# The S5 front of an encoder kernel: zero-led Toeplitz strips issued by one queue, the discretisation split over two engines, x loaded in quarters

## The reference

```python
def s5_mixer(u, lam_re, lam_im, log_step, b_re, b_im, c_re, c_im, d, glu_w, glu_b):
    ...
    step = jnp.exp(log_step.astype(f32))[:, None]
    lam_bar = jnp.exp(lam * step)
    b = lax.complex(b_re.astype(f32), b_im.astype(f32))
    b_bar = ((lam_bar - 1.0) / lam)[..., None] * b
    bu = jnp.einsum('blgn,gpn->blgp', uf.astype(jnp.complex64), b_bar)
    a = jnp.broadcast_to(lam_bar, (1, seq, S5_GROUPS, S5_STATE))
    _, states = lax.associative_scan(_linear_recurrence_combine, (a, bu), axis=1)
    c = lax.complex(c_re.astype(f32), c_im.astype(f32))
    y = jnp.einsum('gnp,blgp->blgn', c, states).real + d.astype(f32) * uf
    y = jax.nn.gelu(y.reshape(bsz, seq, D_MODEL))
    y = y * jax.nn.sigmoid(y @ glu_w.astype(f32) + glu_b.astype(f32))
```

## Time and profile before

| what | value |
|---|---|
| median of 3 runs (range) | 1308.99 us (1308.8 to 1311.32) |
| profiled execution, its own time | 1309.56 us |
| its span, first to last instruction | 1307.8 us |
| PE busy | 1253.6 us, 96% |
| DVE, ACT, POOL busy | 694.8, 465.5, 58.1 us |
| first GLU product starts | 123.78 us into the span |

### The profile page before, as it was taken

How to read it: one execution, slowest core, us unless ns; L and a number is a source line. 1 busy time by engine, 2 the same in 40 slices (tenths; PEclk the granted TensorE clock), 3 DMA queues, 4 the chain that set the end, 5 groups by cost and what they waited for, 6 DMA issues and landing times.

```text
span 1307.8 us, 16043 instructions
## 1 busy us (share of the span) xinstructions
PE 1253.6 (96%) x6253; PEld 1039.9 (80%) x6253; DVE 694.8 (53%) x822; ACT 465.5 (36%) x481; POOL 58.1 (4%) x64
## 2 busy tenths in 40 slices
PE   2779999999999999999999999999999999999997
PEld 2768778888887888888888888888788888887886
DVE  8797874444444445555556464554355454444433
ACT  4834544242423333324223332332233232323222
POOL 2960000000000000000000000000000000000000
PEclk9989999999999999999999999999999999999999
DMA  5053323333322323322313223233332323222231
GB/s 112 2 136 100 96 88 105 96 96 96 96 86 81 96 88 114 103 100 96 105 33 121 79 65 103 65 96 96 97 97 88 104 90 102 90 72 89 88 101 73
DMA packets 147791, 119.18 MB, mean 91 GB/s; under 512 B 12857, under 2 KB 140017, under 8 KB 147761
## 3 DMA queue, kind: packets, MB, share of 16 engines
q1 hardware_dynamic: 143584, 115.78, 28.5%
q10 hardware_dynamic: 4176, 2.98, 1.1%
HBM read 114.29 MB, written 2.10 MB: 89 GB/s over the span
## 4 chain that ended last, share of the span: by engine, by line
PE 89%; DVE 4%; ACT 3%; issue 1%; DMA 1%; ACTq 1%; SPq 0%; DVEq 0%
PE bank L673 25%; PE bank L675 25%; PE bank L674 25%; PE bank L769 2%; PE bank L770 2%; PE bank L771 2%; PE bank L780 1%; ACTq L398 1%; DVE w_lo L1126 1%; PE bank L797 1%; PE bank L795 1%; PE bank L796 1%; DVE tmp L1116 1%; DMA w_raw<-in_s_glu_w_dram 1%; PE bank L625 1%
## 5 line engine op out<-in xcount | busy, mean ns | idle before, releaser
L673 PE MATMUL bank<-u_hi,w_hi 128*128 128x512 f32 x960 | 375.5, 391 | 2.0 <-DVE xT L1390 1.1
L675 PE MATMUL bank<-u_hi,w_lo 128*128 128x512 f32 x960 | 374.0, 390 | 0.0
L674 PE MATMUL bank<-u_lo,w_hi 128*128 128x512 f32 x960 | 373.8, 389 | 0.0
L1126 DVE TENSOR_TENSOR w_lo<-w_raw,w_hi 128x2048 fp32r<-128x2048 f32 x112 | 256.7, 2292 | 200.2 <-ACT w_hi L850 199.8
L850 ACT ACTIVATE w_hi<-w_raw 128x2048 fp32r<-128x2048 f32 x112 | 213.5, 1906 | 188.6 <-PE bank L675 146.4
L673 PEld LDWEIGHTS bank<-u_hi,w_hi 128*128 128x128 f32 x960 | 180.3, 188 | 40.5 <-issue 2.0
L675 PEld LDWEIGHTS bank<-u_hi,w_lo 128*128 128x128 f32 x960 | 180.3, 188 | 37.6
L674 PEld LDWEIGHTS bank<-u_lo,w_hi 128*128 128x128 f32 x960 | 180.3, 188 | 37.4 <-issue 0.5
L673 PE MATMUL bank<-h_hi,w_hi 128*128 128x512 f32 x352 | 137.3, 390 | 2.8 <-DVE w_lo L1126 2.8
L674 PE MATMUL bank<-h_lo,w_hi 128*128 128x512 f32 x352 | 137.1, 389 | 0.0
L675 PE MATMUL bank<-h_hi,w_lo 128*128 128x512 f32 x352 | 137.0, 389 | 0.0
(11 more groups left out here) (199 smaller groups left out, 1352.2 us busy)
## 6 DMA issues: line engine op xcount, KB each, us to landing
w_raw<-in_ret_w_qkvg_dram SPq DMA_DIRECT2D x24, 1024.0 KB, 5.0
w_raw<-in_ffn_w_gate_dram SPq DMA_DIRECT2D x22, 1024.0 KB, 5.1
w_raw<-in_ffn_w_up_dram SPq DMA_DIRECT2D x22, 1024.0 KB, 5.1
w_raw<-in_ffn_w_down_dram SPq DMA_DIRECT2D x32, 704.0 KB, 4.2
w_raw<-in_ret_w_o_dram SPq DMA_DIRECT2D x8, 1024.0 KB, 5.1
w_raw<-in_s_glu_w_dram SPq DMA_DIRECT2D x4, 1024.0 KB, 6.0
s<-in_x_dram ACTq DMA_DIRECT2D x2, 1024.0 KB, 12.2
s_w<-in_x_dram SPq DMA_DIRECT2D x1, 2048.0 KB, 10.0
```

Of the source, the lines that this page charges most:

```text
L673: pe.matmul(o, w_hi[w][:, w_cols], hi, start=first, stop=False)
L674: pe.matmul(o, w_hi[w][:, w_cols], lo, start=False, stop=False)
L675: return pe.matmul(o, w_lo[w][:, w_cols], hi, start=False, stop=end)
L1126: dve.tensor_tensor(w_lo[s][:, :], w_raw[:, s, :], w_hi[s][:, :].bitcast(F32), ALU.subtract).then_inc(w_lo_ready[s], 1)
```

## The change

It changes how the same values are made, and no arithmetic of the layers.

- **Strips with zeros ahead.** `strip` gets 448 zeros (LEAD = 7*16*4) ahead of each block's 512 values, written once by POOL. The four pairs of a block are interleaved: element m of pair i lies at 4m + i. One DMA now copies [16 partitions, 2 blocks, 512 contiguous elements], always 64 KB, from a start that lies 64r elements further left for block row r. Strips 4 to 7 lie on partitions 32 to 63. `zero_toeplitz` is gone. `y_inputs` reads `toep` with a step of four elements.
- **All 64 DMAs on SyncE.** Part 0 is issued before the load of x for the residual, parts 1 and 2 after it, then the load of GLU weights into slot 0, then part 3.
- **Front.** DVE gives out rows 3 and 4 first and begins with the powers; f is made by POOL (with DVE's reciprocal) and transposed in a fill of its own; POOL also multiplies the powers by f, copies for the segment powers, and prepares the diagonal after its first block.
- **x in quarters.** ACT issues 8 DMAs instead of 2, and squares four steps of x before `fb`, two after, two after f. The table of Sqrt is loaded ahead, and so is that of gelu.
- **Order.** PE transposes the second half table before `u`; strips 0 and 1 stand in the table loop, 2, 7, 3 and 4 before the transposes of x, 5 after, 6 after `y_inputs(3)`. `y_inputs(0)` no longer waits for the scan (`Y_BANK`). DVE copies the last part of C by itself.

```diff
-        def toeplitz_half(queue, part, half):
-
-            queue.wait_ge(toep_zeroed, 2 * part + 2)
+        def toeplitz(queue, part):
+
             for k in (2 * part, 2 * part + 1):
                 b, fill = S5_AT[("strip", k)]
                 queue.wait_ge(bank_free[b], fill + 1)
-            js = slice(PART * part, PART * part + PART)
-            gs = slice(J * half + js.start, J * half + js.stop)
-            for r in range(STEPS):
-                queue.dma_start(toep[N * r:N * r + N, gs, N * r:P],
-                                strip[N * half:N * half + N, js, 0:P - N * r]).then_inc(toep_loaded[part], 16)
+            for half in range(2):
+                row = 2 * N * (part // 2) + N * half
+                for r in range(STEPS):
+                    at = LEAD - N * JB * r
+                    queue.dma_start(toep[N * r:N * r + N, half, 2 * part:2 * part + 2, :],
+                                    strip[row:row + N, part % 2, :, at:at + P * JB]).then_inc(toep_loaded[part], 16)
...
+            sp.wait_ge(pads_zeroed, 1)
+            toeplitz(sp, 0)
+
             b, fill = S5_AT[("tb", 4 * NTAB - 1)]
             sp.wait_ge(bank_full[b], fill + 1)
             sp.wait_ge(tb_ready, 2 * NTAB)
             sp.wait_ge(tc_last_ready, 1)
             sp.dma_start(x_tok, x[0].rearrange("(t p) d -> p t d", p=P)).then_inc(x_loaded, 16)
 
-            toeplitz_half(sp, 0, 0)
-            toeplitz_half(sp, 0, 1)
-            toeplitz_half(sp, 1, 0)
-            toeplitz_half(sp, 2, 0)
-            for part in range(2):
+            toeplitz(sp, 1)
+            toeplitz(sp, 2)
+            for part in (0, 2):
                 sp.wait_ge(toep_loaded[part], 16 * 2 * STEPS)
             load_unit(0, 0, glu_v[:, :, 0:256], KT, 256)
-            toeplitz_half(sp, 3, 0)
-            for part in range(2, 4):
+            toeplitz(sp, 3)
+            for part in (1, 3):
                 sp.wait_ge(toep_loaded[part], 16 * 2 * STEPS)
             load_unit(1, 0, glu_v[:, :, 256:512], KT, 256)
...
             s5_tables(0, 0)
+            s5_tables(0, 1)
             pe.wait_ge(xn_ready, STEPS)
             for k in range(8):
                 s5_steps(k)
-            s5_tables(0, 1)
...
-                    pe.matmul(o, u[:, jj, half, :], toep[:, J * half + jj, :], start=(jj % 4 == 0), stop=False)
-
+                    pe.matmul(o, u[:, jj, half, :], toep[:, half, jj // JB, jj % JB::JB],
+                              start=(jj % 4 == 0), stop=False)
+
+            pe.wait_ge(toep_loaded[0], 16 * 2 * STEPS)
+            y_inputs(0)
+            y_inputs(1)
+            pe.wait_ge(seg_done, 1)
+            pe.wait_ge(toep_loaded[1], 16 * 2 * STEPS)
+            y_inputs(2)
+            y_inputs(3)
+            strips(6)
             pe.wait_ge(seg_done, 2)
-            for k in range(4):
-                if k % 2 == 0:
-                    pe.wait_ge(toep_loaded[k // 2], 16 * 2 * STEPS)
-                y_inputs(k)
-            strips(6)
+            keep_clock(s5_open("y", 6)[0], 8)
...
             s5_table_out(0, 0)
+            act.wait_ge(rs_ready, 1)
+            for t in range(STEPS):
+                act.activation(xn[:, :, t, :], xc[:, t, :].rearrange("p (j n) -> p j n", j=J), ACT.Copy,
+                               scale=small[:, 16 + t:17 + t]).then_inc(xn_ready, 1)
+            s5_table_out(0, 1)
             for k in range(8):
                 s5_steps_out(k)
-            s5_table_out(0, 1)
...
-            step(mul(row(5), row(21), row(18)))
-            mul(row(6), row(23), row(18)).then_inc(rows_ready, 1)
-
+            mul(row(4), row(7), row(11)).then_inc(rows_ready, 1)
+            dve.wait_ge(rows_ready, 1)
```

More of the change, by code:

```diff
@@ L305, in trunk @@
         vecs_loaded = sem("vecs_loaded")
-        xc_loaded = sem("xc_loaded")
+        xc_loaded = [sem(f"xc_loaded{q}") for q in range(4)]
         c_loaded = sem("c_loaded")
@@ L540, in _ @@
             pe.wait_ge(rows_ready, 1)
-            for i in range(4):
+            for i in range(2):
                 mm = pe.transpose(ps[:, J * i:J * i + J], rows[:, 3 + i, :], ident[0:J, 0:J])
+            mm.then_inc(full, 1)
+            ps, full = s5_open("f", 0)
+            pe.wait_ge(f_ready, 1)
+            for i in range(2):
+                mm = pe.transpose(ps[:, J * i:J * i + J], rows[:, 5 + i, :], ident[0:J, 0:J])
             mm.then_inc(full, 1)
@@ L568, in _ @@
                 s5_steps(k)
-            s5_tables(0, 1)
+            ps, full = s5_open("vec", 0)
+            pe.wait_ge(vecs_loaded, 6 * 16)
+            pe.transpose(ps[:, 0:NVEC], vec_rows, ident[64:64 + NVEC, 64:64 + NVEC]).then_inc(full, 1)
             def strips(k):
@@ L594, in _ @@
                     pe.wait_ge(diag_ready, 1)
-                    strips(0)
+                if c >= 2:
+                    strips(c - 2)
                 s5_tables(c, 1)
@@ L868, in _, with x_square @@
             act.activation(rows[:, 12, :], rows[:, 10, :], ACT.Sin, scale=0.5).then_inc(sin_ready, 1)
+            act.activation(small[:, 26:27], eps[:, :], ACT.Sqrt)
+            def x_square(t):
+                if t % 2 == 0:
+                    act.wait_ge(xc_loaded[t // 2], 32)
+                if t:
+                    act.wait_ge(ms_ready, t)
+                act.activation(junk, xc[:, t, :], ACT.Square, accum_out=small[:, t:t + 1]).then_inc(ms_ready, 1)
+            for t in range(4):
+                x_square(t)
             act.wait_ge(fb_zeroed, 1)
@@ L875, in _ @@
                     copy(fb[rows64, ri, :, N * half:N * half + N], bt_gained[ri][rows64]).then_inc(fb_ready, 1)
[L876 to L880, removed]
+            x_square(4)
+            x_square(5)
+            ps, free = s5_full("f", 0)
+            copy(lam_t[:, 2:4, :], ps[:, 0:2 * J].rearrange("p (r j) -> p r j", r=2)).then_inc(free, 1)
+            x_square(6)
+            x_square(7)
             ps, free = s5_full("ms", 0)
             act.activation(small[:, 8:16], ps[:, 0:STEPS], ACT.Sqrt, bias=eps[:, :], scale=1.0 / D).then_inc(free, 1)
-            ps, free = s5_full("vec", 0)
-            copy(vecs[:, :], ps[:, 0:NVEC]).then_inc(free, 1)
             for ri in range(2):
@@ L888, in _ @@
                 copy(ct[:, ri, :, :].rearrange("p j n -> p (j n)"), ps[:, :], -1.0 if ri else 1.0).then_inc(free, 1)
-            act.wait_ge(rs_ready, 1)
-            for t in range(STEPS):
-                act.activation(xn[:, :, t, :], xc[:, t, :].rearrange("p (j n) -> p j n", j=J), ACT.Copy,
-                               scale=small[:, 16 + t:17 + t]).then_inc(xn_ready, 1)
             def s5_table_out(c, ri):
@@ L1219, in complex_mul @@
                 settle()
-            step(dve.memset(powers[:, 0, 0, :], 1.0))
             step(dve.memset(powers[:, 1, 0, :], 0.0))
@@ L1269, in _ @@
                         dve.reciprocal(small[:, 16:24], small[:, 8:16]).then_inc(rs_ready, 1)
-            dve.wait_ge(ct_copied, 2)
+            for ri in range(2):
+                b, fill = S5_AT[("ct", ri)]
+                dve.wait_ge(bank_free[b], fill + 1)
+                step(dve.tensor_copy(ct_last[:, ri, :, :], ct[:, ri, J - JB:J, :]))
+            settle()
+            dve.wait_ge(c_powers_ready, 1)
             js = slice(J - JB, J)
@@ L1618, in _ @@
             pool.memset(fb[:, :, :, :], 0.0).then_inc(fb_zeroed, 1)
+            pool.memset(strip[:, :, :, 0:LEAD], 0.0).then_inc(pads_zeroed, 1)
             pool.wait_ge(ident_loaded, 16)
@@ L1639, in segment_powers @@
             def segment_powers():
+                step(pool.tensor_copy(seg_powers[:, :, 0, :], powers[:, :, STEPS, :]))
+                settle()
                 for have in (1, 2, 4):
@@ L1655, in _ @@
             for k in range(NBLK - 1):
+                if k == 1:
+                    diagonal()
                 if k == 2:
```

159 lines of the change are left out of this document (81 added, 78 removed).

## The result

The changed kernel takes 1313.62 us (median of 8 runs, 1312.21 to 1315.8) against 1309.84 us (8 runs, 1308.8 to 1311.5) of the kernel before beside it: ratio 1.0028, 95% interval 1.0017 to 1.0039. It is slower, where 1303.9 us, faster, was forecast, and it lies outside the range of 1298 to 1310. The first GLU product starts at 129.71 us instead of 123.78; what follows takes 1314.0 - 129.71 = 1184.3 us, and took 1307.8 - 123.78 = 1184.0. So all of the loss, 5.9 us here and 3.8 us in the medians, lies ahead of that product, as the prediction assumed.

What follows compares the result with a forecast made beforehand. It took the first GLU product's start, set by the last Toeplitz DMA rather than the scan, as the bound: 123.8 - 118.7 = 5.1 us gained, 1309.56 to 1304.5, median 0.57 lower, 1303.9 us; range 1298 to 1310.

Steps and rivals of the forecast that it cites:

- an issue on SyncE, put at 0.60 us: Toeplitz DMAs on SyncE: each issue taken at 0.60 us, between 0.47 and 0.65, so 9.6 us per part of 16.
- the stepped read, taken as 0: `y_inputs(6)` and `(7)`: reading `toep` at a 16-byte step costs 0 to 80% of 1.97 us; 0 was taken.
- The Toeplitz chain: Strips and DMAs before the first GLU product: part 3 lands at 105.0 us, 5.1 before the old 110.1; GLU at 118.7.
- SP becomes the bound, slower: Rival, SyncE's row: 48 issues cost 0.23 us more each, 11 us; GLU at 129.7, time 1315 us; chance 0.12.
- The stepped read costs: Rival, `y_inputs(6)` and `(7)`: 3.5 to 3.9 us instead of 1.97, 1305.7 us; chance 0.16 shared with a late front.
- The front: DVE's start: rows earlier, f product to POOL, one copy gone; 5.2 us saved, tables from 19.65 instead of 24.84 us.
- ACT's strip copies: ACT carrying strips out of PE: strip 1 out about 0.9 us after PE, strip 5 0.6 us after.
- PE's 0.9 us more for `u`: PE's products for `u` in the front: taken at 5.15 us, as in the kernel before.
- The half tables: DVE's table stretch: each half table takes 3.65 us, so the first is there at 23.3 us.
- The last gap: Behind `y_inputs(6)`, up to the first GLU product: stretch of 13.7 us, nothing changing in length.

Runs made afterwards that it cites:

- e2: The changed kernel, but ACT issues half 1 of parts 2 and 3 (16 of the 64 DMAs): 1309.06 us, ratio 0.9995 to the kernel before.
- e1: The changed kernel with pairs' strips not interleaved, so writes and reads are contiguous: 1312.72 us, ratio 1.0023 to the kernel before.
- e5: The changed kernel with contiguous strips and half 1 of parts 2 and 3 issued by ACT: 1303.2 us, ratio 0.995 to the kernel before.
- e8: The changed kernel with contiguous strips, plus 14 filling products on PE ahead of its wait for part 3: 1309.87 us, ratio 1.0001 to the kernel before.
- e9: The changed kernel, but POOL starts f only after DVE's powers, and f's transposes and copy follow those of C: 1316.3 us, one run.
- e4: The changed kernel, but the transposes of y for k 4 and 5 go to banks 6 and 7: 1313.41 us, ratio 1.0028 to the kernel before.
- e10: e7 with half of part 1 issued by ACT too, behind its copy of strip 3: 1307.11 us, ratio 0.9982 to the kernel before.
- e3: The changed kernel, but SP issues the load of x for the residual ahead of part 0: 1311.83 us, ratio 1.0017 to the kernel before.
- e7: e5 plus the edits of e3 and e4, x transposed ahead of strip 4 and filling products on PE: 1301.41 us, ratio 0.9933 to the kernel before.

## Why the prediction was wrong

The order of the chain held, and the lengths of its pieces didn't. The steps that failed are three terms: an issue on SyncE, put at 0.60 us, measured at 0.72 over the 48 on the chain; the stepped read, taken as 0, with 1.9 us more measured behind part 3; and PE's clock, which the text left out, 1.9 us in the transposes of x. Forecast and measured length of each piece, in us:

| piece | forecast | measured | late |
|---|---|---|---|
| to the first table | 19.65 | 21.02 | 1.4 |
| on to `u` done | 16.35 | 17.44 | 1.1 |
| on to the first issue of part 0 | 16.0 | 16.26 | 0.3 |
| part 0, 16 issues | 9.6 | 11.25 | 1.7 |
| x until PE has it | 10.0 | 9.32 | -0.7 |
| transposes of x | 5.0 | 6.93 | 1.9 |
| strip 5 and its copy | 2.8 | 3.40 | 0.6 |
| part 2 until landed | 12.1 | 12.43 | 0.3 |
| weights, part 3 until landed | 13.5 | 15.21 | 1.7 |
| from `y_inputs(6)` to the last transposes | 13.7 | 15.58 | 1.9 |
| bank wait | 0 | 0.87 | 0.9 |
| sum | 118.7 | 129.71 | 11.0 |

The measured column is of the slowest of eight executions: the median missed the forecast by 9.7 us, not by 11.0.

- **The Toeplitz chain, the step of the 0.60 us an issue.** The median issue is 0.594 us, and one follows the next after 0.635. But single ones took 1.38, 1.39 and 2.63 us in the parts on the chain, and part 3's 16 took 12.97 us, 0.81 each. The 48 took 34.6 us (0.72 each), 5.2 more than forecast; 1.5 of it came back, since the sum adds landings of 2.5 and 2.7 us behind the end of the last issue, while the rows count it from that issue's start. The rival *SP becomes the bound, slower* named this place, with 0.76 as its point. The three series together cost 3.7 us more than forecast (1.7, 0.3 and 1.7), not the 11 of its price (which by its own row, 4.77 / 6 = 0.80 and not 0.83, is 9.4). That its 129.7 us for the first GLU product is the measured figure is luck. e2 shows, by 4.6 us in the medians and 7.8 in the traces, that the row of issues is what the end waits for. What holds up the single issues is not shown. Their cost isn't size: 32 rows of 2 KB and 128 of 512 bytes cost the same.
- **The stepped read, taken as 0.** It was a bound in the text, at 1.6 to 2 us; its size was right for `y_inputs(6)` and `(7)` (3.89 against 1.97), and it was the rival *The stepped read costs*. But e1 shows that at this place the lower clock would have cost the same 1.9 us without it. The two don't add there: undoing the step alone leaves 3.68 us.
- **What the prediction left out altogether: the clock.** It has no term for it. A longer wait of PE, 4.88 us for POOL's block 4 and 3.94 for part 3, brought the lower level behind it. Strip 4 took 3.62 instead of 1.94 us, which was not on the chain, as PE waited 1.79 us for x behind it; but the clock stayed down, and the transposes of x took 6.93 us at a mean of 0.56 instead of 5.15 at 1.00 in e5. In the last stage of e1, e8 puts 2.6 us on it. No rival held it.
- **The front.** The forecast 5.2 us on DVE were 3.8. Of the 1.4, 0.85 are POOL's work beside small DVE products (e9), a cost that the text put at nothing for f.
- **ACT's strip copies.** They write with the same step of 16 bytes and take 1.08 instead of 0.59 us. Strip 5's was taken at 0.6, strip 1's at 0.9.
- **PE's 0.9 us more for `u`**: 6.05 us instead of 5.15, at a granted clock of 1.00. No run shows its cause. The eight transposes of each half table ahead of it, from 24.66 and 28.40 us on, took 1.97 us at a shown 1.00 too, where eight take 1.94 at 0.50 in e1 and 1.09 at 1.00 elsewhere; so in this early stretch the granted clock of the rows doesn't tell how long a product takes.
- **The half tables**: (61.12 - 3.67 - 24.84 - 3.17) / 8 is 3.68 and not 3.65 us, which moves nothing on the chain.
- **The last gap**, 0.86 us: the text called the stretch behind `y_inputs(6)` unchanged in length, and before no such wait stood there. e4 shows that it is the bank.
- **What was right**: that all turns on the start of the first GLU product, that the scan ends long before the last Toeplitz DMA, that part 3 is what PE waits for, and the order x, strip 5, part 2, part 3.

Small errors, all but one of one sign, on one chain of eleven pieces made 11 us; the forecast gain was 5.1. The change won 6.4 us on DVE, which was not what the first GLU product waited for, and paid on the chain that it did wait for, where the 24 issues that ACT had made came to stand in one row with SyncE's 40.

## What to carry to other kernels

When many small DMAs move onto one queue, count each at its period including the stalls (0.66 to 0.81 us here, not the median of 0.594), and lay half of what is on the chain on a second engine that has nothing to do in that stretch: e5, with contiguous reads as well, is 0.5% faster than the kernel before, while e2, the second queue alone, only equals it. Count on a later landing with two queues. And measure it in its place: in e10, where ACT took half of part 1 too, an issue cost double and 5.7 us were lost. Undo costs in pairs before calling one harmless: the stepped read was worth 0.9 us while the queue bounded and 5.9 us (1309.06 to 1303.2) once it didn't. Where a change gives PE a new wait, price what follows it at the lower clock as well.

## What was not expected of the hardware

- A moving operand read with a step of 16 bytes doubles a product of 128 columns at the full clock (116 against 58 ns) and costs little at half (3.90 us in e3, 3.68 without the step in e1, per 32, both at 0.50).
- PE's waits of 3.9 to 4.9 us in the changed kernel were each followed by a stretch at the lower level, whereas it stood at 1.00 behind the one of 1.47 us in e5. In e7 it was at 0.50 in 68.5 to 70 us, behind waits of 0.68 and 1.08 us with eight short products between them.
- With two queues the last DMA of part 2 landed 4.9 to 5.1 us after its issue (e5, e7), with one after 2.42 us.
- Two queues issuing side by side cost 0.60 to 0.69 us an issue each in one stretch, and 1.2 to 1.3 each in another of nearly the same kernel (e7, e10).
- GpSimd's work on 32 partitions beside DVE's products of 128x64 made a pair of them take 0.62 instead of 0.36 us.
